# The three products of a split-weight chunk in another order: low weights by high input first, low input last

## The chip, the core and the metric

One core of one Trainium2 chip runs the whole program. The metric is device time in microseconds (us) of one execution. Besides it there is one execution recorded by the hardware profiler, from which all rows below are read. TensorE is called PE in these rows, its weight loads PEld, VectorE DVE, ScalarE ACT, GpSimd POOL, and SyncE, which starts most transfers, SP.

## What is computed

One decoder layer for 256 prompt tokens and 8 single-token sequences, 264 columns in all, in float32:

```python
ada = (c @ w_ada + b_ada)[:, None, :]
sh1, sc1, g1, sh2, sc2, g2 = jnp.split(ada, N_ADA, axis=-1)
u = x * (1 + sc1) + sh1
proj = u @ w_in                                   # 2048 x 8192
z_p, x_c, b_c, c_c, gate_p, gate_c = jnp.split(proj, [o1, o2, o3, o4, o5], axis=-1)
y_p, new_pool = _pool_mixer(z_p, pool_hist, pos, pool_grp_w, pool_scale)
y_p = y_p @ w_pool_up                             # 1024 x 2048
y_c, new_conv = _short_conv(c_c * x_c, conv_hist, conv_w)
y_c = (b_c * y_c) @ w_conv_up                     # 1024 x 2048
mixed = (jax.nn.sigmoid(gate_p) * y_p + jax.nn.sigmoid(gate_c) * y_c) @ w_o   # 2048 x 2048
x = _layernorm(ALPHA * x + g1 * mixed, ln1_g, ln1_b)
u2 = x * (1 + sc2) + sh2
h = jnp.square(jax.nn.relu(u2 @ w_ff1 + b_ff1))   # 2048 x 8192
x = _layernorm(ALPHA * x + g2 * (h @ w_ff2 + b_ff2), ln2_g, ln2_b)            # 8192 x 2048
```

The outputs are the new x of the prompt and of the samples, and the last rows of the pooling and the convolution inputs as new state.

## The kernel before

**Split products.** PE multiplies in a type (float32r) that keeps fewer bits than float32. So each weight tile and each input tile is held as two parts: the high part is the value rounded to that type, the low part is what is left. A product of a weight chunk by an input tile is then three PE products that add up in PSUM: high by high, high by low, low by high. The helper `three` (lines 1590 to 1595) issues them. Each is one weight load of 128 x 128 and one matmul of 128 x 264.

**Units.** The weights are taken in units of 4 chunks (128 rows of the contraction each) by 512 output columns, 1 MB. SP loads a unit into one of four slots of `raw`; ACT writes the high part to `w_hi` (line 715), DVE the low part to `w_lo` (line 1005), each with two slots; PE then runs the helper `unit` (lines 1605 to 1621): for each of 4 output tiles m, which have a PSUM bank each, it runs over the 4 chunks c and calls `three` for each. That makes 4 x 4 x 3 = 48 products in a unit. PE waits once for a unit, for `unit_split`, which DVE raises when both parts are there, and at a bank's first product for `psum_free`. The last of the products of an output tile raises `part_done`, by which DVE or ACT may read the bank, and after the fourth tile ACT and DVE may overwrite the slots.

**Inputs.** An input tile is 264 floats, 1056 bytes, in each partition. `U`, `M` and `H` hold 32, 16 and 32 of them; `M` lies over the upper tiles of `U`. `H` begins 32 tiles behind `U`. The low tile that belongs to a high tile lies:
- 4 tiles further (4224 bytes) for the input projection w_in and for w_ff1, which together make 2 x 64 x 16 = 2048 chunks;
- 8, 16 or 24 tiles away (8448 bytes or a multiple) for the pooling groups, the two up-projections, w_o and w_ff2, which make 16 + 2 x 128 + 256 + 1024 = 1552 chunks.

The first two chunks of the input projection are written out by hand (`first_pair`, lines 1669 to 1687), so that `three` is called for 3598 chunks.

**Stages.** PE runs the conditioning products and the input projection, the pooling groups, the up-projections, w_o, the first normalisation, and then four times 4 blocks of w_ff1 and 4 blocks of w_ff2, each block being 4 units; the second normalisation and the output end it. In a block of w_ff1 the first unit runs in `first_chunks` (lines 1977 to 1987), which goes over the chunks outside and over the output tiles inside. All other units go over output tiles outside. A block of w_ff2 reads input tiles 0 to 3, 4 to 7, 8 to 11 and 12 to 15 of `H` in its four units.

The order of PE's instructions is that in which they are written, in loops of the sequencer.

Of the kernel before, what the change touches and what calls it, by code (L numbers as in the profile page):

```python
# [120 lines left out]
def build_layer(nc, a, o):  # L121
    with ExitStack() as ctx:
# [1464 lines left out]
        def _(pe):  # L1587
            mm = nc.tensor.matmul

            def three(out, w, x_hi, x_lo, start, stop):  # L1590

                wh, wl = w
                mm(out, wh, x_hi, start=start, stop=False)  # L1593
                mm(out, wh, x_lo, start=False, stop=False)  # L1594
                return mm(out, wl, x_hi, start=False, stop=stop)  # L1595

            def w_of(s, c, m, width=UC):

# [6 lines left out]
            def unit(j, n, t0, hi, lo, first=True, last=True, early=None, pieces=None):  # L1605

                if not pieces:
                    pe.wait_ge(unit_split, split_done(n))  # L1610
                for m in range(MT):
                    if pieces:
                        pe.wait_ge(pieces, m + 1)
                    if early and m == MT - 1:
                        early()
                    if first:
                        pe.wait_ge(psum_free, bank_free(t0 + m))
                    for c in range(KC):
                        r = three(bank[m][:, 0:TOK], w_of(j % HL, c, m), tile_of(hi[0], hi[1] + c),
                                  tile_of(lo[0], lo[1] + c), first and c == 0, last and c == KC - 1)  # L1620
                    r.then_inc(part_done, 1)
# [47 lines left out]
            def first_pair():  # L1669

                w = [w_of(0, c, e, HW) for e in range(2) for c in range(2)]
                acc = [bank[e][:, 0:TOK] for e in range(2)]
                pe.wait_ge(u_samples, 1)
                pe.wait_ge(u_hi_ready, 1)
                pe.wait_ge(half_hi, 1)
                for e in range(2):
                    mm(acc[e], w[2 * e][0], U[:, 0, :], start=True, stop=False)
                pe.wait_ge(lo_pieces, 1)
                for e in range(2):
                    mm(acc[e], w[2 * e][1], U[:, 0, :], start=False, stop=False)  # L1680
                pe.wait_ge(u_tile, 1)
                for e in range(2):
                    mm(acc[e], w[2 * e][0], U[:, KC, :], start=False, stop=False)
                pe.wait_ge(u_ready, 1)
                for e in range(2):
                    r = three(acc[e], w[2 * e + 1], U[:, 1, :], U[:, KC + 1, :], False, True)
                r.then_inc(part_done, 1)

            def half_unit(n):

                h = n // HU
                if n == 0:
                    first_pair()
                else:
                    pe.wait_ge(u_ready, h + 1)
                for p in range(1 if n == 0 else 0, PAIRS):
                    pe.wait_ge(lo_pieces, PAIRS * n + p + 1)
                    if PAIRS * n + p >= 2:
                        pe.wait_ge(psum_free, pair_free(PAIRS * n + p))
                    for e, c in ((e, c) for e in range(2) for c in range(2)):  # L1700
                        r = three(bank[p % 2 * 2 + e][:, 0:TOK], w_of(n % HL, c, 2 * p + e, HW), U[:, 2 * h + c, :],
                                  U[:, KC + 2 * h + c, :], c == 0, c == 1)
                    r.then_inc(part_done, 1)
                    if n == 2:
                        hist_sums((2 * p, 2 * p + 1))
# [400 lines left out]
```

## Time and profile before

| what | before |
|---|---|
| median of 3 runs | 1456.91 us (1456.75 to 1457.5) |
| the profiled execution's own time | 1457.35 us |
| its span, first to last instruction | 1455.4 us |
| mean granted PE clock | 0.998 of full speed |
| PE busy | 1438.6 us, 99% of the span, 12268 matmuls |
| weight loads | 1370.0 us, 94%, 12268 loads |
| DVE, ACT, POOL busy | 853.0, 528.3 and 102.5 us |

The mean length of one matmul in the groups of instructions (283 to 285 ns) is from its start to its modelled end; matmuls overlap in the engine, so what a product costs PE is the distance from one start to the next. That is read from the timeline, whose starts are given to 0.01 us: over 48 products that is 0.2 ns for each.

### The profile page before, as it was taken

How to read it: one execution, taken by the hardware profiler on the slowest of the kernel's cores; microseconds unless marked ns; L12 is line 12 of the kernel's file. 1: busy time of each engine (PE TensorE's matmuls, PEld its weight loads, DVE VectorE, ACT ScalarE, POOL GpSimd, SP SyncE). 2: the span in 40 equal slices, each digit the busy share in tenths (PEclk: the TensorE clock that was granted, in tenths of full speed). 3: DMA queues.
4: the chain of work that ended last, by engine and by line, in shares of the span. 5: the costliest groups of instructions: out<-in, count | busy, mean ns of one | idle time of the engine just before them, and what ended most of it. 6: DMA issues, size and time to landing. Idle time of an engine off the chain costs nothing.

```text
span 1455.4 us, 28268 instructions
## 1 busy us (share of the span) xinstructions
PE 1438.6 (99%) x12268; PEld 1370.0 (94%) x12268; DVE 853.0 (59%) x1036; ACT 528.3 (36%) x380; POOL 102.5 (7%) x102
## 2 busy tenths in 40 slices
PE   7999999999999999999999999999999999999998
PEld 6999999998889889897899999999999999999997
DVE  4777666565688656459754545454445544454557
ACT  2333322323335232225534333443334433343435
POOL 1000000000440000000060000000000000000800
PEclk9999999999999999999999999999999999999999
DMA  9988888887886786886765555655556545655541
GB/s 318 382 296 281 300 324 306 308 325 270 328 311 253 279 329 244 338 298 240 248 204 186 189 173 176 180 189 177 175 180 187 179 174 180 187 180 173 182 165 61
DMA packets 150529, 344.71 MB, mean 237 GB/s; under 512 B 6452, under 2 KB 17240, under 8 KB 142105
## 3 DMA queue, kind: packets, MB, share of 16 engines
q1 hardware_dynamic: 148642, 340.36, 68.1%
q0 software_dynamic: 896, 2.36, 0.5%
q8 instruction: 61, 1.00, 0.3%
q10 hardware_dynamic: 912, 0.85, 0.2%
q14 instruction: 18, 0.15, 0.0%
HBM read 341.24 MB, written 2.79 MB: 236 GB/s over the span
## 4 chain that ended last, share of the span: by engine, by line
PE 96%; DVE 2%; DMA 1%; ACT 0%; issue 0%; SPq 0%; DVEq 0%; ACTq 0%
PE main L1593 30%; PE main L1594 30%; PE main L1595 30%; PE ps_ada L1711 1%; PE ps_adat L1711 1%; PE ps_adat L1757 1%; PE ps_a L1711 1%; DMA PB<-in_w_ada 1%; PE ps_ada L1757 1%; DVE w_lo L1005 0%; PE ps_ada L1662 0%; SPq L439 0%; DVE G L1452 0%; PE ps_ada L1649 0%; ACT w_hi L715 0%
## 5 line engine op out<-in xcount | busy, mean ns | idle before, releaser
L715 ACT ACTIVATE w_hi<-raw 128x2048 fp32r<-128x2048 f32 (+1 forms) x227 | 429.7, 1894 | 884.5 <-PE main L1595 871.6
L1005 DVE TENSOR_TENSOR w_lo<-raw,w_hi 128x2048 fp32r<-128x2048 f32 (+1 forms) x212 | 483.3, 2280 | 451.2 <-ACT w_hi L715 450.6
L1593 PE MATMUL main<-U,w_hi 128*128 128x264 f32 x2318 | 660.9, 285 | 3.0 <-issue 1.3
L1595 PE MATMUL main<-U,w_lo 128*128 128x264 f32 x2318 | 658.1, 284 | 0.0
L1594 PE MATMUL main<-U,w_hi 128*128 128x264 f32 x2190 | 619.6, 283 | 0.0
L1593 PEld LDWEIGHTS main<-U,w_hi 128*128 128x128 f32 x2318 | 435.6, 188 | 25.8 <-issue 22.2
L1595 PEld LDWEIGHTS main<-U,w_lo 128*128 128x128 f32 x2318 | 435.0, 188 | 0.0
L1594 PEld LDWEIGHTS main<-U,w_hi 128*128 128x128 f32 x2190 | 411.6, 188 | 0.0
L1593 PE MATMUL main<-H,w_hi 128*128 128x264 f32 x1280 | 364.8, 285 | 0.0
L1595 PE MATMUL main<-H,w_lo 128*128 128x264 f32 x1280 | 362.2, 283 | 0.0
L1594 PE MATMUL main<-H,w_hi 128*128 128x264 f32 x1152 | 327.3, 284 | 0.0
L1593 PEld LDWEIGHTS main<-H,w_hi 128*128 128x128 f32 x1280 | 240.8, 188 | 3.5 <-issue 3.4
L1595 PEld LDWEIGHTS main<-H,w_lo 128*128 128x128 f32 x1280 | 240.4, 188 | 0.0
L1594 PEld LDWEIGHTS main<-H,w_hi 128*128 128x128 f32 x1152 | 216.7, 188 | 0.1
L1594 PE MATMUL main<-M,w_hi 128*128 128x264 f32 x256 | 72.8, 284 | 0.0
L1236 DVE TENSOR_TENSOR PB<-main,PB 128x264 f32<-128x264 f32 x96 | 38.3, 427 | 32.8 <-PE main L1595 32.7
L1236 DVE TENSOR_TENSOR G<-main,G 128x264 f32<-128x264 f32 x96 | 37.6, 427 | 27.2 <-PE main L1595 27.1
L1594 PEld LDWEIGHTS main<-M,w_hi 128*128 128x128 f32 x256 | 48.2, 188 | 0.1
L676 POOL MEMSET Uf<- 128x528 f32 x1 | 0.5, 543 | 594.4 <-PE main L1595 594.4
L1098 DVE TENSOR_TENSOR w_lo<-raw,w_hi 128x512 fp32r<-128x512 f32 x60 | 40.7, 682 | 0.5 <-ACT w_hi L715 0.5
L1352 DVE SCALAR_TENSOR_TENSOR X<-main,ada,X 128x256 f32<-128x256 f32 x72 | 34.1, 480 | 2.4 <-PE main L1595 1.4
L592 POOL TENSOR_TENSOR Uf<-Uf 128x2040 f32<-128x2040 f32 (+3 forms) x4 | 9.4, 2360 | 336.6 <-ACT Uf L817 336.2
(280 smaller groups left out, 636.7 us busy)
## 6 DMA issues: line engine op xcount, KB each, us to landing
raw<-in_w_ff SPq DMA_DIRECT2D x128, 1024.0 KB, 5.2
raw<-in_w_in SPq DMA_DIRECT2D x63, 1024.0 KB, 9.4
ada_raw<-in_w_ada SPq DMA_DIRECT2D x48, 1024.0 KB, 6.6
ada_raw<-in_w_ada SPq DMA_DIRECT2D x36, 512.0 KB, 6.4
raw<-in_w_o SPq DMA_DIRECT2D x16, 1024.0 KB, 9.7
Uf<-in_w_ada SPq DMA_DIRECT2D x10, 1024.0 KB, 10.6
Uf<-in_w_ada SPq DMA_DIRECT2D x16, 512.0 KB, 7.6
raw<-in_w_pool_up SPq DMA_DIRECT2D x8, 1024.0 KB, 9.3
```

Of the source, the lines that this page charges most:

```text
L592: g_tt(dst[:, first:PT, step:PROMPT], src[:, first:PT, step:PROMPT], src[:, first:PT, 0:PROMPT - step], ALU.add)
L676: nc.gpsimd.memset(sum_x, 0.0).then_inc(sum_zeroed, 1)
L715: nc.scalar.activation(w_hi[:, s % HL, 0:size], raw[:, s, 0:size], ACT.Copy).then_inc(hi_ready, 1)
L1005: tt(w_lo[:, s % HL, 0:size], raw[:, s, 0:size], w_hi[:, s % HL, 0:size].bitcast(F32), ALU.subtract).then_inc(unit_split, 1)
L1098: tt(lo, r, hi.bitcast(F32), ALU.subtract).then_inc(lo_pieces, 1)
L1236: tt(dst, bank[m][:, 0:TOK], dst, ALU.add).then_inc(psum_free, 1)
L1352: stt(xt, bank[m][:, 0:PROMPT], gt[:, 0:1], xt, ALU.mult, ALU.add)
L1593: mm(out, wh, x_hi, start=start, stop=False)
L1594: mm(out, wh, x_lo, start=False, stop=False)
L1595: return mm(out, wl, x_hi, start=False, stop=stop)
L1711: r = mm(section_bank[i][BLOCK * j:BLOCK * j + BLOCK, :], c_t[:, k, C_AT:C_AT + BLOCK], blocks[:, j], start=k == 0, stop=k == NT - 1)
L1757: r = mm(group_bank[t][BLOCK * j:BLOCK * j + BLOCK, 0:GROUP_COLS], c_t[:, 2 * n + c, C_AT:C_AT + BLOCK], blocks[:, c, j], start=n == 0 and ...
```

## The change

`three` issues the same three products of the same operands in another order. Before: high weights by high input, high weights by low input, low weights by high input. After: low weights by high input, high weights by high input, high weights by low input. The flags that open and close a sum in PSUM go to the first and the last product as before, and so does the signal at the end of an output tile, which the caller attaches to the product that `three` returns.

```diff
             def three(out, w, x_hi, x_lo, start, stop):
 
                 wh, wl = w
-                mm(out, wh, x_hi, start=start, stop=False)
-                mm(out, wh, x_lo, start=False, stop=False)
-                return mm(out, wl, x_hi, start=False, stop=stop)
+                mm(out, wl, x_hi, start=start, stop=False)
+                mm(out, wh, x_hi, start=False, stop=False)
+                return mm(out, wh, x_lo, start=False, stop=stop)
```

PE's first calls of `three`, at the start of the input projection; each row is a matmul, its output, its input and weights, and what it waits for. Before:

```order
L1593 MATMUL main<-U,w_hi 128x264 [waits u_ready]
L1594 MATMUL main<-U,w_hi 128x264
L1595 MATMUL main<-U,w_lo 128x264
L1593 MATMUL main<-U,w_hi 128x264
L1594 MATMUL main<-U,w_hi 128x264
L1595 MATMUL main<-U,w_lo 128x264
L1593 MATMUL main<-U,w_hi 128x264 [waits lo_pieces]
```

After:

```order
L1593 MATMUL main<-U,w_lo 128x264 [waits u_ready]
L1594 MATMUL main<-U,w_hi 128x264
L1595 MATMUL main<-U,w_hi 128x264
L1593 MATMUL main<-U,w_lo 128x264
L1594 MATMUL main<-U,w_hi 128x264
L1595 MATMUL main<-U,w_hi 128x264
L1593 MATMUL main<-U,w_lo 128x264 [waits lo_pieces]
```

The product with the low weights moved from the third place to the first; the waits stay at the first place. `lo_pieces` is raised by DVE when a piece of the low weights is written, which comes after the high part.

PE at the start of a unit of the convolution's up-projection, where high and low input lie in two tensors (`U` and `H`). Before:

```order
L1593 MATMUL main<-U,w_hi 128x264 [waits psum_free,unit_split,yc_ready]
L1594 MATMUL main<-H,w_hi 128x264
L1595 MATMUL main<-U,w_lo 128x264
L1593 MATMUL main<-U,w_hi 128x264
L1594 MATMUL main<-H,w_hi 128x264
L1595 MATMUL main<-U,w_lo 128x264
```

After:

```order
L1593 MATMUL main<-U,w_lo 128x264 [waits psum_free,unit_split,yc_ready]
L1594 MATMUL main<-U,w_hi 128x264
L1595 MATMUL main<-H,w_hi 128x264
L1593 MATMUL main<-U,w_lo 128x264
L1594 MATMUL main<-U,w_hi 128x264
L1595 MATMUL main<-H,w_hi 128x264
```

The two products with the high input from `U` now stand side by side, and the one with the low input from `H` closes the chunk. The rows of DVE, ACT, POOL and SP are the same before and after, and on PE the number of rows, the lines and the waits at each place too.

## Rows read from the trace of the kernel before

**Rows 1.** The page's head and its first two parts.

```profile
span 1455.4 us, 28268 instructions
PE 1438.6 (99%) x12268; PEld 1370.0 (94%) x12268; DVE 853.0 (59%) x1036; ACT 528.3 (36%) x380; POOL 102.5 (7%) x102
PEclk9999999999999999999999999999999999999999
```

**Rows 2.** The page's chain of work that ended last, by engine.

```profile
PE 96%; DVE 2%; DMA 1%; ACT 0%; issue 0%; SPq 0%; DVEq 0%; ACTq 0%
```

**Rows 3.** Waits: engine, its line, releaser: us in total, times, longest.

```profile
ACT w_hi L715 <- PE main L1595: 871.6, 218, 7.7
DVE w_lo L1005 <- ACT w_hi L715: 450.6, 180, 5.6
PE main L1593 <- DVE w_lo L1005: 1.0, 2, 0.8
```

**Rows 4.** Groups of instructions from the page: busy us, mean ns, idle before.

```profile
L1593 PE MATMUL main<-U,w_hi 128*128 128x264 f32 x2318 | 660.9, 285 | 3.0 <-issue 1.3
L1595 PE MATMUL main<-U,w_lo 128*128 128x264 f32 x2318 | 658.1, 284 | 0.0
L1594 PE MATMUL main<-U,w_hi 128*128 128x264 f32 x2190 | 619.6, 283 | 0.0
L1593 PEld LDWEIGHTS main<-U,w_hi 128*128 128x128 f32 x2318 | 435.6, 188 | 25.8 <-issue 22.2
```

**Rows 5.** Timeline, second w_ff1 stage, third unit of its second block: start us, length.

```profile
921.01 0.28 PE L1593 MATMUL main<-U,w_hi 128*128 128x264 f32 x1
921.01 0.19 PEld L1594 LDWEIGHTS main<-U,w_hi 128*128 128x128 f32 x1
921.13 0.28 PE L1594 MATMUL main<-U,w_hi 128*128 128x264 f32 x1
921.13 0.19 PEld L1595 LDWEIGHTS main<-U,w_lo 128*128 128x128 f32 x1
...
921.38 0.29 PE L1593 MATMUL main<-U,w_hi 128*128 128x264 f32 x1
...
921.74 0.28 PE L1593 MATMUL main<-U,w_hi 128*128 128x264 f32 x1
...
922.09 0.28 PE L1593 MATMUL main<-U,w_hi 128*128 128x264 f32 x1
...
922.46 0.28 PE L1593 MATMUL main<-U,w_hi 128*128 128x264 f32 x1
```

**Rows 6.** Timeline: first products of w_ff1 units, second stage; 48 products between unit starts.

```profile
880.23 0.28 PE L1593 MATMUL main<-U,w_hi 128*128 128x264 f32 x1
...
886.05 0.29 PE L1593 MATMUL main<-U,w_hi 128*128 128x264 f32 x1
...
903.50 0.28 PE L1593 MATMUL main<-U,w_hi 128*128 128x264 f32 x1
...
909.37 0.28 PE L1593 MATMUL main<-U,w_hi 128*128 128x264 f32 x1
...
915.20 0.28 PE L1593 MATMUL main<-U,w_hi 128*128 128x264 f32 x1
...
926.82 0.28 PE L1593 MATMUL main<-U,w_hi 128*128 128x264 f32 x1
```

**Rows 7.** Timeline: the same of w_ff2 units, second stage, and the next w_ff1 start.

```profile
973.46 0.28 PE L1593 MATMUL main<-H,w_hi 128*128 128x264 f32 x1
...
996.76 0.28 PE L1593 MATMUL main<-H,w_hi 128*128 128x264 f32 x1
...
1002.56 0.28 PE L1593 MATMUL main<-H,w_hi 128*128 128x264 f32 x1
...
1008.41 0.28 PE L1593 MATMUL main<-H,w_hi 128*128 128x264 f32 x1
...
1014.21 0.28 PE L1593 MATMUL main<-H,w_hi 128*128 128x264 f32 x1
...
1020.05 0.28 PE L1593 MATMUL main<-H,w_hi 128*128 128x264 f32 x1
...
1066.64 0.28 PE L1593 MATMUL main<-U,w_hi 128*128 128x264 f32 x1
```

## Prediction

> **What bounds the kernel now.** I read the page's head first: PE is busy for 1438.6 of 1455.4 us, at a granted clock in the top tenth in all forty slices, the 2.4 GHz level [rows 1]. The chain that ended last is PE for 96% [rows 2]. The waits say who is ahead: ACT waits for PE to free a slot of the high weights for 871.6 us in 218 waits, DVE waits behind ACT for 450.6, while PE waited for DVE's low weights for 1.0 us, twice [rows 3]. So weights arrive early everywhere, and the time is the sum of what PE's products cost one after the other. For a change inside `three` the question is only what one product costs, and whether it depends on which product stands before it.
>
> The groups give 283 to 285 ns for a matmul at each of the three lines [rows 4], but these overlap. The timeline shows the true distance: matmuls start 0.12 us apart, and the weight load of the next product starts together with the matmul of the one before, also when it loads the same high weights again (921.01 for line 1594) [rows 5]. A load is recorded for every product, the repeated ones too; nothing is skipped (x12268 of both) [rows 1]. From one unit's first product to that of the next there are 48 products. A stage of w_ff1 takes 973.46 - 880.23 = 93.23 us for 768 products, 121.4 ns each; one of w_ff2 1066.64 - 973.46 = 93.18 us, 121.3 ns each [rows 6, 7]. The 10,794 products of `three` (3 x 3598) at 121.4 ns are 1310 us of the 1455.4; the other 145 us are conditioning products, transposes, the few stalls and the two ends, none of which the change touches.
>
> **The change, part by part.** (a) *Number and kind of instructions.* Three loads and three matmuls before and after, of the same shapes, the same weights read twice in a row once per chunk in both orders: before, high weights in places 1 and 2; after, in places 2 and 3. Nothing added, nothing taken away: 0 us.
>
> (b) *Waits.* A unit waits once, at its first product, for both parts of the weights, and the same wait stands there after. In the order before, the high-weight product could in principle have started ahead of the low weights, but it did not: the wait covered both. Where the weights are taken in pieces, at the start of the input projection, `lo_pieces` is again waited for ahead of all three. So DVE's lateness (1.0 us in 2 waits [rows 3]) is paid as before: 0 us. Even if a wait grew by its whole present size again it would be 1 us. The last product of a tile still raises `part_done` at the same place in the stream, so banks and slots come free at the same time, and SP's, ACT's and DVE's queues see the same releases: 0 us. What hides ACT and DVE is their lead on PE of hundreds of microseconds in sum; a change of 0.24 us in when the low weights are read within a chunk does not touch it.
>
> (c) *The spacing of products.* This is the one unknown term. It would be nothing if every product cost the same. It does not. In a unit of w_ff1 the chunks take 0.37, 0.36, 0.35 and 0.37 us in turn (921.01, 921.38, 921.74, 922.09, 922.46) [rows 5]. In w_ff2 the units take 1002.56 - 996.76 = 5.80, then 5.85, 5.80 and 5.84 us, that is 120.8, 121.9, 120.8 and 121.7 ns a product [rows 7]; all are free of waits. The units alternate with the input tiles they read: units one and three read tiles 0 to 3 and 8 to 11, two and four tiles 4 to 7 and 12 to 15. Eight tiles are 8448 bytes, 33 x 256; four tiles are 4224, which leaves 128 over. So I take it, as an estimate from these rows, that the spacing depends on where the input tile lies within some 256 bytes, and on little else.
>
> With that the chunks fall into two classes. For 1552 chunks (4656 products: groups, up-projections, w_o, w_ff2) high and low input lie a multiple of 8 tiles apart, and high and low weights are 16 KB apart. Seen in this way all three products of a chunk read the same places, and the new order is the old one: 0 us. For the 2046 chunks left (6138 products: w_in and w_ff1) the low tile is 128 bytes off. The places read were (a, a+128, a) and become (a, a, a+128): the same three, in another sequence. If a product's cost goes by its own place, the sum stays. The rows support that: two parts of the 120.8 level and one of 121.8 give (2 x 120.8 + 121.8) / 3 = 121.1 ns, and a steady w_ff1 unit pair shows 926.82 - 915.20 = 11.62 us for 96 products, 121.0 [rows 6]. After the change the mixture is the same. I take 0 us for (c).
>
> Bounds from both sides: if the sequence matters, the level could go anywhere that wait-free units show. The lowest is 120.8 [rows 7], which for 6138 products would give (120.8 - 121.1) x 6138 = -1.8 us. The highest is the first unit of the second w_ff1 block, 909.37 - 903.50 = 5.87 us, 122.2 ns [rows 6], which would give +1.1 x 6138 = +6.8 us. I stay at 0 because the mixture reproduces the measured level without any term for the sequence.
>
> Here a rule of the Trainium skill speaks. The rows show 121.4 ns a product with 264 columns, and a spread with the tile read. "TensorE: Matmul & The Clock Gate", Part 2 (step-by-step, and back-to-back issue gap), says that the array has two independent read ports, so that loading the next weights takes nothing from the running matmul, and puts a matmul at its columns by 2.4 GHz plus about 2.5 ns, 112.5 ns here by my working. By that rule the order could not matter at all; the rows differ from it by 9 ns a product, so something of the two reads does interact, and the measurement decides. That gap is why the slower rival below has a chance.
>
> **The rivals.** *Slower: the same input tile twice in a row costs more.* After the change two neighbouring products read the same high tile. Before, this happened only in the unit that goes over chunks outside and output tiles inside, where the last product of one `three` and the first of the next share it. That unit is the slow one in the second block, 5.87 us. Against it: the same unit in the first block of the stage took 886.05 - 880.23 = 5.82 us, 121.2 ns [rows 6], with the same sequence of tiles, so the slow level comes from how the unit is entered, not from the repeat. And w_ff2 units, whose three products all read like places, are not slow. Price +6.8 us: 1463.7. It decides the sign of the result once the spacing grows by 0.5 ns in those 6138 products (3 us).
>
> *Faster: the new sequence falls into the short spacing more often.* One chunk in four of a w_ff1 unit takes 0.35 us, the others 0.36 to 0.37 [rows 5], so a better sequence exists. Were it one chunk more in each four, that is 2046 / 4 = 512 chunks by some 15 ns, -7.7 us: 1449.2. The extreme, all at 0.35 us, is 2046 x 13 ns = -27 us. For it speaks only that nothing rules it out; against it, the mixture argument again.
>
> *The change doesn't do what it says,* or does nothing but reorder: that is the forecast itself. The order of instructions shows the swap in place and no other row moved. A gain from loading the high weights only once would need the second load to vanish; in the kernel before, two neighbouring products had the same weights as well and both loads are there [rows 5], so I give it nothing.
>
> **How the numbers follow.** The sum is made against the profiled execution: 1457.35 us, of which 1455.4 is the span and 1.95 lies around it, 0.44 above the median of 1456.91. The change adds 0 + 0 + 0 us to any of them, so I predict the median, 1456.9. A measurement of this kernel can tell about 0.2% from no change, 2.9 us: 1454.0 to 1459.8. Chances: no difference 0.81; slower by the sequence 0.12; faster by the sequence 0.07. Both ends in term (c) are inside what could happen, and the upper one lies further out, so the range reaches higher than lower: 1453.8 to 1461.0. That holds the forecast's case whole and the weaker half of the slower one.
>
> **What the profile of the changed kernel would show.** For (a): line 1593 with `w_lo`, lines 1594 and 1595 with `w_hi`, the counts of groups unchanged, 12268 loads. For (b): PE's waits for DVE still a microsecond or so, and ACT's wait for PE near 870 us, now under the same line 1595. For (c): w_ff2 units at 5.80 and 5.85 us in turn, unchanged to 0.01 us, since their places are the same; a stage of w_ff2 at 93.18 us. A stage of w_ff1 at 93.2 us within 0.4 (0.5 ns a product). The prediction is wrong if a w_ff1 stage takes 94 us (the slower rival), or 92.4 (the faster one), and the idea of places within 256 bytes falls if w_ff2's units move by more than 0.02 us.

## The result and the profile after

| what | before | after |
|---|---|---|
| median of 22 runs each | 1457.99 us | 1459.74 us |
| ratio after / before | | 1.0014, 95% interval 1.0008 to 1.0019 |
| span of the profiled execution | 1455.4 us | 1457.1 us |

The change makes the kernel slower by 0.14%, 1.75 us at the medians: less than the 0.2% inside which the forecast counted a result as no change, but more than the interval of the ratio leaves to chance. The profiled executions differ by 1.7 us. The rhythm of a unit of products repeats to 0.01 us from unit to unit and from trace to trace, so the traces can say where these are.

The page's head and first parts, and the granted clock, of the changed kernel (answers to [rows 1]); then the waits (answers to [rows 3]), with us in total, times and longest:

```profile
span 1457.1 us, 28268 instructions
PE 1440.1 (99%) x12268; PEld 1371.7 (94%) x12268; DVE 852.7 (59%) x1036; ACT 528.3 (36%) x380; POOL 102.5 (7%) x102
PEclk9999999999999999999999999999999999999999
```

```profile
ACT w_hi L715 <- PE main L1595: 872.8, 218, 7.7
...
PE main L1593 <- DVE w_lo L1005: 1.0, 2, 0.7
```

The same work, the same clock, the same microsecond of waiting for DVE. PE is simply busy for 1.5 us longer. The starts of products in the timeline show in which stage. Four places before: first whole unit of the input projection, first pooling group, first w_ff1 unit, and the last product of the layer.

```profile
123.30 0.29 PE L1593 MATMUL main<-U,w_hi 128*128 128x264 f32 x1
...
461.43 0.28 PE L1593 MATMUL main<-U,w_hi 128*128 128x264 f32 x1
...
688.54 0.36 PE L1593 MATMUL main<-U,w_hi 128*128 128x264 f32 x1 [1.29 <-issue]
...
1440.24 0.28 PE L1595 MATMUL main<-H,w_lo 128*128 128x264 f32 x1
```

The same four places after:

```profile
123.21 0.28 PE L1593 MATMUL main<-U,w_lo 128*128 128x264 f32 x1
...
462.63 0.29 PE L1593 MATMUL main<-U,w_lo 128*128 128x264 f32 x1
...
689.75 0.36 PE L1593 MATMUL main<-U,w_lo 128*128 128x264 f32 x1 [1.44 <-issue]
...
1441.94 0.28 PE L1595 MATMUL main<-H,w_hi 128*128 128x264 f32 x1
```

- Up to the first row: -0.09 us. The first call of `three` comes 1.16 us earlier (22.94 against 24.09 us), and most of that is lost again by this row. In the traces of the ten kernels that carry out the whole layer it lies between 23.9 and 24.3 us in the four with the inputs in the order of before, and between 22.2 and 25.5 in the six with that of after. So single traces differ by more than this at their start.
- Input projection, 50 units, 2400 products: 338.13 us before, 339.42 after, **+1.29**.
- Groups, up-projections, w_o, first normalisation: 227.11 and 227.12, **0.01**.
- w_ff1 and w_ff2: 751.70 and 752.19, **+0.49**.

Within the feed-forward part the second stage shows the units; w_ff1 first (answers to [rows 6]), then w_ff2 (answers to [rows 7]).

```profile
881.57 0.28 PE L1593 MATMUL main<-U,w_lo 128*128 128x264 f32 x1
...
904.90 0.29 PE L1593 MATMUL main<-U,w_lo 128*128 128x264 f32 x1
...
910.72 0.28 PE L1593 MATMUL main<-U,w_lo 128*128 128x264 f32 x1
...
916.56 0.29 PE L1593 MATMUL main<-U,w_lo 128*128 128x264 f32 x1
...
928.24 0.29 PE L1593 MATMUL main<-U,w_lo 128*128 128x264 f32 x1
...
974.92 0.29 PE L1593 MATMUL main<-H,w_lo 128*128 128x264 f32 x1
...
998.22 0.28 PE L1593 MATMUL main<-H,w_lo 128*128 128x264 f32 x1
...
1004.02 0.28 PE L1593 MATMUL main<-H,w_lo 128*128 128x264 f32 x1
...
1009.87 0.28 PE L1593 MATMUL main<-H,w_lo 128*128 128x264 f32 x1
...
1068.10 0.28 PE L1593 MATMUL main<-U,w_lo 128*128 128x264 f32 x1
```

The stage of w_ff2 takes 93.18 us, as before, and its units 5.80 and 5.85, as before. In w_ff1 a steady pair of units takes 928.24 - 916.56 = 11.68 us, 121.7 ns a product, against 121.0 by the rows of before. The first unit of a block goes the other way: 5.82 us, 121.2 ns, against 5.87 (in the first block of a stage, where it took 5.82 before, it now takes 5.81). Together a stage takes 93.35 in place of 93.23. The change cost 0.6 ns a product in w_ff1's steady units, those that follow another unit of their kind. It gave 1 ns back in the first unit of three blocks out of four, and did nothing in w_ff2.

In the input projection the changed kernel has two levels. Here are the starts of two pairs of neighbouring units, the same code on the same layout, with no wait between:

```profile
189.65 0.29 PE L1593 MATMUL main<-U,w_lo 128*128 128x264 f32 x1
...
195.49 0.29 PE L1593 MATMUL main<-U,w_lo 128*128 128x264 f32 x1
...
216.80 0.28 PE L1593 MATMUL main<-U,w_lo 128*128 128x264 f32 x1
...
222.67 0.28 PE L1593 MATMUL main<-U,w_lo 128*128 128x264 f32 x1
```

The first pair lies 5.84 us apart, 121.7 ns a product, the second 5.87 (5.866 before rounding), 122.2 ns. Of the 50 units 22 run at 121.7 ns and 10 at 122.2; the others come behind conditioning products or, one of them, after a short pause, and average more. A level holds until the next conditioning products. In the kernel before, all 30 units that settle do so at 121.1 ns. So in the changed kernel one sequence has two steady rhythms, and the +1.29 us is a mixture of +0.6 and +1.1 ns a product.

### The profile page after: what moved, and what is told of

It reads as the page before. It is cut to its first block, busy times and chain, and to the rows that moved or that the text cites. A ratio compares the mean times of both kernels' runs of the same rounds, so it can differ in the third digit from the quotient of the medians.

```text
span 1457.1 us, 28268 instructions
## 1 busy us (share of the span) xinstructions
PE 1440.1 (99%) x12268; PEld 1371.7 (94%) x12268; DVE 852.7 (59%) x1036; ACT 528.3 (36%) x380; POOL 102.5 (7%) x102
## 4 chain that ended last, share of the span: by engine, by line
PE 95%; DVE 2%; SPq 1%; DMA 1%; ACT 1%; issue 0%; DVEq 0%; ACTq 0%
PE main L1593 30%; PE main L1594 29%; PE main L1595 29%; PE ps_ada L1711 1%; PE ps_adat L1711 1%; PE ps_adat L1757 1%; PE ps_a L1711 1%; DMA raw<-in_w_in 1%; SPq L439 1%; PE ps_ada L1757 1%; DVE w_lo L1005 0%; ACT w_hi L715 0%; PE ps_ada L1662 0%; DVE G L1452 0%; SPq L443 0%
## 5 line engine op out<-in xcount | busy, mean ns | idle before, releaser
L1593 PE MATMUL main<-U,w_lo 128*128 128x264 f32 x2318 | 665.1, 287 | 3.5 <-issue 1.4
```

What stands on the lines that cost most here:

```text
L1593: mm(out, wl, x_hi, start=start, stop=False)
```

## The experiments

**Which of the two sequences matters, weights or inputs?** The change alters both: the weights from (high, high, low) to (low, high, high), the inputs from (high, low, high) to (high, high, low). Two kernels take them apart; each edit is shown against the kernel before.

```diff
-                mm(out, wh, x_hi, start=start, stop=False)
+                mm(out, wl, x_hi, start=start, stop=False)
                 mm(out, wh, x_lo, start=False, stop=False)
-                return mm(out, wl, x_hi, start=False, stop=stop)
+                return mm(out, wh, x_hi, start=False, stop=stop)
```

> Order of the three products: low weights by high input, high weights by low input, high weights by high input. The weights come in the order of the changed kernel, the inputs (high, low, high) in that of the kernel before. Theory A (the spacing goes by the sequence of the places of the input tiles alone): the spacing of the kernel before to 0.01 us, that is first w_ff1 unit of a block 5.86 us, a steady one 5.81, a w_ff1 stage 93.2 us, and a time within 0.5 us of before. Theory B (the spacing goes by which weights come first): the spacing of the changed kernel, first unit 5.81 us, steady ones 5.84, a w_ff1 stage 93.4 us, time +1.5 to 2 us. w_ff2 units 5.80 and 5.85 us by both.

Measured: ratio to before 1.0004 (0.9995 to 1.0013). Unit starts of the second w_ff1 stage:

```profile
880.12 0.28 PE L1593 MATMUL main<-U,w_lo 128*128 128x264 f32 x1
...
903.40 0.28 PE L1593 MATMUL main<-U,w_lo 128*128 128x264 f32 x1
...
909.26 0.28 PE L1593 MATMUL main<-U,w_lo 128*128 128x264 f32 x1
...
915.09 0.28 PE L1593 MATMUL main<-U,w_lo 128*128 128x264 f32 x1
...
926.72 0.28 PE L1593 MATMUL main<-U,w_lo 128*128 128x264 f32 x1
...
973.36 0.28 PE L1593 MATMUL main<-H,w_lo 128*128 128x264 f32 x1
```

First unit 5.86, steady pair 11.63, stage 93.24 us: the kernel before, with the low weights first.

```diff
                 mm(out, wh, x_hi, start=start, stop=False)
-                mm(out, wh, x_lo, start=False, stop=False)
-                return mm(out, wl, x_hi, start=False, stop=stop)
+                mm(out, wl, x_hi, start=False, stop=False)
+                return mm(out, wh, x_lo, start=False, stop=stop)
```

> Order: high weights by high input, low weights by high input, high weights by low input. The inputs come as in the changed kernel (high, high, low), the weights as in neither, and no two neighbouring products of a chunk share weights. Theory A (places of the inputs alone): the spacing of the changed kernel to 0.01 us, first w_ff1 unit 5.81, steady ones 5.84, stage 93.4 us, time +1.5 to 2 us on before. Theory B (which weights come first): the spacing of before, 5.86, 5.81, stage 93.2, time within 0.5 us of before. Theory C (two neighbouring products with the same weights are dearer or cheaper than others): a third spacing, in w_ff2 too.

Measured: ratio 1.0016 (1.0007 to 1.0025).

```profile
881.31 0.28 PE L1593 MATMUL main<-U,w_hi 128*128 128x264 f32 x1
...
904.65 0.29 PE L1593 MATMUL main<-U,w_hi 128*128 128x264 f32 x1
...
910.46 0.28 PE L1593 MATMUL main<-U,w_hi 128*128 128x264 f32 x1
...
916.31 0.29 PE L1593 MATMUL main<-U,w_hi 128*128 128x264 f32 x1
...
927.99 0.29 PE L1593 MATMUL main<-U,w_hi 128*128 128x264 f32 x1
...
974.67 0.29 PE L1593 MATMUL main<-H,w_hi 128*128 128x264 f32 x1
```

First unit 5.81, steady pair 11.68, stage 93.36: the changed kernel, with the high weights first; its input projection has the changed kernel's two levels too. A stage of w_ff2 takes 93.18 us in both kernels. Theories B (weights) and C (repeated weights) fall, and A stands: the sequence of the inputs does it alone. The order of the weights has no effect in this kernel, where high and low weights lie 16 KB apart.

**Do other engines or transfers have a part in it?** A kernel of PE products only, on data that lie still. The core of the helper behind each of its tests; `pairs` and `times` give the 48 products and their repeats:

```python
for m, c in pairs * times:                       # 4 output tiles by 4 chunks, 48 products
    hi, lo = places(c)
    for k, (w, i) in enumerate(order):           # BEFORE = hh, hl, lh   AFTER = lh, hh, hl
        s = (0 if w == "h" else US) + (0 if w_fixed else c * 512 + m * P) + w_shift // 4
        x = (hi if i == "h" else lo) // 4
        mm(bank[m][:, 0:cols], w_all[:, s:s + P], x_all[:, x:x + cols], start=c == 0 and k == 0, stop=c == 3 and k == 2)
```

> Only PE products of 128 x 264 on weights and inputs that lie still, no layer: everything else is left out and the outputs are zeros. Groups of 48 products, one source line for each test: the orders of before, after and the two mixed ones with the low tile 4 tiles (4224 bytes) away, then 8 tiles away, then all inputs at one place (0, 32, ... 224 bytes past a multiple of 256), weights moved by 32, 64 and 128 bytes, the same weights throughout, 256 and 128 columns, and chunks outside. Theory A: without any other engine at work the orders give 121.1 (before) and 121.7 ns (after) as in the kernels, the mixed order with inputs high, low, high the first and with high, high, low the second; 8 tiles away both orders give the same, 120.8 (tiles 0 to 3) and 121.9 (tiles 4 to 7). Single places differ from one another by some ns, between 117 and 125. Theory D (the difference comes from traffic of other engines or transfers beside PE): all orders alike here, and nearer to 117 than to 121.

Its timeline, one row for each test: start, length, line, number of products. L119 is the order of before, L120 that of after, L121 inputs high, low, high with low weights first, L122 inputs high, high, low with high weights first.

```profile
29.29 17.60 PE L119 MATMUL main<-x_all,w_all 128*128 128x264 f32 x144
46.73 17.75 PE L120 MATMUL main<-x_all,w_all 128*128 128x264 f32 x144
64.31 17.64 PE L121 MATMUL main<-x_all,w_all 128*128 128x264 f32 x144
81.80 17.75 PE L122 MATMUL main<-x_all,w_all 128*128 128x264 f32 x144
```

The length of a row runs to the end of its last product, 0.16 us past the next product's start; less that, 17.44, 17.59, 17.48 and 17.59 us for 144 products, 121.1, 122.2, 121.4 and 122.2 ns. With nothing else at work the order of before has its level of the kernel, and the inputs' sequence orders the four (L121 carries a transient from L120 in its first unit). Theory D falls. The size that the expectation gave for the order of after, 121.7 ns, was missed: it is 122.2 here, the level that w_ff1's units of the changed kernel don't have and ten units of its input projection have.

The same run has units whose low tile is 8 tiles away, high and low then a multiple of 256 bytes apart (L123 to L126). Tiles 0 to 3 settle at 5.81 us, 121.1 ns, and tiles 4 to 7 at 5.85, 121.9, in the order of before and in that of after alike. So the 5.80 us of w_ff2's units in the kernel, 120.8 ns, is not the steady level of their place: it is what they cost in turn with the others.

All inputs at one place, two units (96 products) each: L127 at a multiple of 256 bytes, L128 32 bytes further, L131 128, L132 160; L143 has 256 columns, L144 128 columns.

```profile
146.01 11.69 PE L127 MATMUL main<-x_all,w_all 128*128 128x264 f32 x96
157.53 11.84 PE L128 MATMUL main<-x_all,w_all 128*128 128x264 f32 x96
...
192.29 11.81 PE L131 MATMUL main<-x_all,w_all 128*128 128x264 f32 x96
203.94 11.89 PE L132 MATMUL main<-x_all,w_all 128*128 128x264 f32 x96
...
331.90 11.68 PE L143 MATMUL main<-x_all,w_all 128*128 128x256 f32 x96
343.41 10.84 PE L144 MATMUL main<-x_all,w_all 128*128 128x128 f32 x96
354.08 11.91 PE L145 MATMUL main<-x_all,w_all 128*128 128x264 f32 x96
```

Less the same 0.16 us, 120.1, 121.7, 121.4 and 122.2 ns for 264 columns, by the place alone (from start to start L127 is 120.0); 119.9 ns (from start to start) for 256 columns at the place that costs 120.0 with 264; 111.1 ns for 128. Eight columns fewer save nothing, and half the columns save 9 ns. So at 256 to 264 columns it is not the columns that set the rhythm.

**The spacing as a function of places.** The same again with whole blocks, the weights' slots and parts where the kernel has them, and all inputs moved.

> PE products alone again, no layer (everything else is left out, the outputs are zeros), now with the weights' two slots and two parts where the kernel has them, and in the sequence of whole blocks: two w_ff1 blocks (first unit chunks outside, input tiles 8j + c, low tiles 4 further), then two w_ff2 blocks (tiles 4j + c, low tiles 16 further). Each test moves all input tiles by 0, 32, ... 224 bytes, in the order of before and of after, or the weights by 64 or 128 bytes, or takes the chunks in another order. Theory A (the spacing is a fixed function of the sequence of places read): at shift 0 the blocks of the kernels come out to 0.02 us, before 23.32 (w_ff1) and 23.30 (w_ff2), after 23.34 and 23.30, and after minus before is 0.2 to 0.6 ns a product in w_ff1's steady units and 0 in w_ff2; other shifts give other levels, some 0.3 to 1 ns lower, and after can be the faster order at some of them. Theory D (other engines' traffic makes the difference): shift 0 misses the kernels' times by more than 0.5 ns a product and the shifts are alike.

Two w_ff1 blocks, 384 products, in each row. L127: order of before, not moved; L131: inputs moved by 64 bytes; L135: by 128; L143: order of after, not moved; L167: order of before, inputs and weights both moved by 128.

```profile
113.95 46.76 PE L127 MATMUL main<-x_all,w_all 128*128 128x264 f32 x384
...
300.55 47.21 PE L131 MATMUL main<-x_all,w_all 128*128 128x264 f32 x384
...
487.78 46.67 PE L135 MATMUL main<-x_all,w_all 128*128 128x264 f32 x384
...
861.13 46.84 PE L143 MATMUL main<-x_all,w_all 128*128 128x264 f32 x384
...
1981.91 46.79 PE L167 MATMUL main<-x_all,w_all 128*128 128x264 f32 x384
```

Less the 0.16 us again. Not moved: 46.60 us for w_ff1 in the order of before and 46.68 in that of after (the kernels: two blocks of 23.32, 46.64, and of 23.34, 46.68; a first block after w_ff2 is 0.05 shorter in the order of before, in the scan as in the kernel). Moved by 64 bytes: 47.05. By 128: 46.50. With inputs and weights moved alike it is nearly as not moved, 46.63, and the second of the two blocks takes 23.32 us in both. The same holds through the scan: for each of the eight moves, the second w_ff1 block with the weights moved by 128 bytes as well takes, to 0.01 us, what it takes with the inputs alone moved by 128 more, counted round 256; and with the weights alone moved by 64 it takes 23.47 us, as with the inputs alone moved by 192. So in this scan what counts is where the input lies relative to the weights, within 256 bytes.

The single places of the first scan fit that only in part. It also moved the weights by 32, 64 and 128 bytes with all inputs at one place. Of these six tests three settle at the level of the same distance without the weights moved, and three don't: 120.0 ns for 121.0, 120.0 for 121.2, and 123.3 for 120.0 (L136, L137, L139). Whether the way in explains these, or the place of the weights counts by itself as well, no run separates.

The order of after is not the dearer one everywhere: by the second w_ff1 blocks of the scan it is the cheaper at moves of 32, 64 and 192 bytes, and the dearer at the other five.

After's steady units now settle at 121.7 ns, as in w_ff1 of the kernel. In the second scan, further down, the same units with the same layout were entered from other products and settled at 122.2. Of the sixteen pairs of move and order that both scans have, fourteen settle at the same level and two don't: this one, and the order of before at 96 bytes (121.7 and 120.6 ns). So one sequence can have more than one steady rhythm, and what stood before it chooses. The changed kernel shows the same two levels in its input projection.

**The scan's numbers put into the kernel.** Four kernels with one line more, the order of before or after, and 32 or 16 floats of room ahead of the input tensors:

```diff
+        sb("shift", [P, 32])
         at_u = here()
         Uf = sb("Uf", [P, 2 * NT, TOK])
```

> The kernel before, order untouched, with 128 bytes of empty room ahead of the input tensors U, H and G, so that every input tile lies 128 bytes further and the weights stay. Theory A (sequence of places, read off the scan): w_ff1 block 23.26 us in place of 23.32, its steady units 120.6 ns a product, w_ff2 units the other way round, 5.85 and 5.80, the block unchanged; in all 16 x -0.067 for w_ff1 and 2440 x -0.55 ns for w_in, -2.4 us, ratio 0.9983. Theory D (other traffic, or layout doesn't matter): no change.

> The kernel before with 64 bytes of room in that place. Theory A: w_ff1 block 16 x +0.22 = +3.5 us, w_in +1.67 ns x 2440 = +4.1, w_ff2 +0.49 ns x 3072 = +1.5, up-projections and w_o +0.75: +9.9 us, ratio 1.007, with w_ff1's steady units at 122.8 ns a product. Theory D: no change.

> The changed kernel with the same 64 bytes. Theory A: w_ff1 +1.2, w_in +1.4, w_ff2, up and w_o +2.3: +4.8 us on the kernel before, so 5 us faster than the order of before at the same place: the change of order is then a gain. Theory B or C (the new order costs by itself, wherever the tiles lie): 2 us slower than the order of before at the same place.

> The changed kernel with 128 bytes. Theory A: w_ff1 +2.45 us, w_in +2.7, the rest 0: +5.2 us on the kernel before, 7.6 us slower than the order of before at the same place. Theory B or C: 2 us slower than that.

| kernel | ratio to before (95%) | expected by A | second w_ff1 block, us: scan, kernel |
|---|---|---|---|
| before, moved by 128 | 0.9977 (0.9968 to 0.9986) | 0.9983 | 23.25, 23.25 |
| before, moved by 64 | 1.0068 (1.0052 to 1.0083) | 1.007 | 23.54, 23.54 |
| after, moved by 64 | 1.0033 (1.0021 to 1.0045) | 1.0033 | 23.39, 23.39 |
| after, moved by 128 | 1.0024 (1.0015 to 1.0034) | 1.0036 | 23.47, 23.47 |

The block's times are the distance between two w_ff1 blocks' first products; for before moved by 64 they can be read here:

```profile
909.65 0.28 PE L1594 MATMUL main<-U,w_hi 128*128 128x264 f32 x1
...
933.19 0.28 PE L1594 MATMUL main<-U,w_hi 128*128 128x264 f32 x1
```

This is the decisive comparison. At 64 bytes the order of after is the faster one, by 5.1 us at the medians (1462.56 against 1467.66); at 128 it is the slower one by 6.7 us (1461.43 against 1454.72); not moved, by 1.75. The new order has no cost of its own: whether it costs or saves depends on where the tiles lie. The last kernel came out 1.4 us short of the expected +5.2; its feed-forward part is exact (+2.5 us). Of the shortfall 0.9 us lies ahead of the first whole unit of the input projection, which it reached at 122.41 us in place of 123.30, and 0.6 in that projection (+2.1 in place of +2.7), which the scan had not imitated. At 64 bytes the projection fell short as well, +3.3 us in place of +4.1 in the order of before and +1.1 in place of +1.4 in that of after, and the start was 0.5 us longer in both: part of the agreement of these two totals is luck. What the scan did imitate came out: the feed-forward part is +5.0 and +2.7 us, as expected. The start varies from trace to trace, as said above; why was not looked into.

**The cheapest sequence.** A second scan over places, orders of the inputs and orders of the chunks.

> PE products alone (no layer; everything else is left out, the outputs are zeros), to look for the cheapest sequence: for the input tiles moved by 0, 32, ... 224 bytes, the six orders of the chunks that begin with chunk 0, and the three orders of a chunk's inputs (high, low, high; high, high, low; low, high, high), three units as w_ff1's later ones each; then four units as w_ff2's for moves 0 to 96 and the six chunk orders. Theory A (a fixed function of the sequence of places): levels spread from about 120 to 123 ns a product, with 120.5 or less for some. The floor is what one place for all gave, 120.0 ns, since 256 columns cost as much as 264 there: the loading of weights sets it. Theory D: no spread.

It found steady levels from 120.0 to 124.4 ns. The only one at 120.0 for the low tile 4 tiles away was this row: the order of after, inputs moved by 192 bytes, chunks 0, 2, 1, 3:

```profile
2063.18 17.45 PE L239 MATMUL main<-x_all,w_all 128*128 128x264 f32 x144
```

17.28 us from its first product to that of the next test, for 144 products. That the loading of weights sets this floor, as the expectation has it, is an inference from 256 and 264 columns costing the same; no run tests it. Built into the kernel, on top of the changed one (shortened: the flag that closes a sum goes to the last chunk of the new order, and `n_is_far` is true for units whose low tile is 4 tiles further):

```diff
+        sb("shift", [P, 48])
...
-                    for c in range(KC):
+                    chunks = (0, 2, 1, 3) if lo[0] is U and hi[0] is U and n_is_far(lo[1], hi[1]) else (0, 1, 3, 2)
+                    for c in chunks:
```

> The cheapest sequence of the second scan put into the kernel: order of the changed kernel (low weights by high input, high by high, high by low), input tensors moved by 192 bytes, chunks in the order 0, 2, 1, 3 in the units whose low tile is 4 tiles further (w_in from its sixteenth unit on, w_ff1's later three units) and 0, 1, 3, 2 in the others; w_ff1's first unit keeps its order. Theory A: if the units settle as in the scan, 120.0 ns in w_in and w_ff1 in place of 121.1: 2440 + 2304 products x -1.1 ns = -5.2 us, others -0.13 ns x 4656 = -0.6, w_ff1's first unit unknown (+-0.8): 1452 +-1, ratio 0.996. If a unit's level hangs on how it is entered, as the scans showed for the changed order at no move (121.7 or 122.2), w_ff1 may settle at another level, up to 122, and the gain is down to that of w_in, or nothing.

> The same with the chunks 0, 2, 1, 3 in w_ff1's first unit too. Theory A: as the kernel without it to 1 us, apart from the level of that unit (768 products) and of what follows it.

The first: ratio 0.9981 (0.9972 to 0.9990), half of what was hoped. The third and fourth units of w_ff1's blocks did reach 120.0 (926.62 - 915.10 = 11.52 us for two units):

```profile
915.10 0.28 PE L1594 MATMUL main<-U,w_lo 128*128 128x264 f32 x1
...
926.62 0.28 PE L1594 MATMUL main<-U,w_lo 128*128 128x264 f32 x1
```

In the input projection nine units reached 120.0 as well, and twenty-one ran at 121.7, so nothing was gained there on the kernel before (338.23 us against 338.13). The second, which differs only in the chunk order of w_ff1's first unit: ratio 1.0008 (0.9999 to 1.0017), its third and fourth units at 121.7 ns; the expectation that it would match the first to 1 us, but for these units, left that open. The two kernels differ by 3.7 us at the medians. Here the same code of a unit runs at 120.0 or 121.7 ns by what ran before it. The two fastest kernels of the study are the kernel before with the inputs moved by 128 bytes (1454.72 us against 1457.59 for before in its comparison, 0.23% faster) and the first of these two (1454.73 against 1457.32); their intervals overlap, so the study doesn't rank them. Both beat both kernels of the case.

## Why the prediction was wrong

**What held.** The bound (PE, product after product) and the view it was read from. Term (a): nothing added or taken away. Term (b): waits, releases and the other engines as before, the wait for the low weights 1.0 us in both. The classes of term (c): for the 4656 products whose parts lie a multiple of 256 bytes apart the forecast was no change to 0.01 us, and it came so in w_ff2, and within 0.01 us over groups, up-projections and w_o together. A w_ff1 stage at 93.35 us also lies within the 0.4 us that the forecast allowed it: the signs of being wrong that it named, 94 and 92.4 us, were set wider than the effect, and so was its 0.2% for what a measurement can tell. With 22 runs of each kernel the interval is 0.05% to either side.

**The step that failed** is the value taken in term (c) for the other 6138 products: "If a product's cost goes by its own place, the sum stays", supported by a mixture of two levels that came to 121.1 ns. It does not go by its own place alone. Two arrangements of the same three places cost 121.1 and 121.7 ns, or 122.2 by the way in. That the mixture hit the level of before was chance. The 120.8 ns that it used is not the level of a place: products alone on tiles 0 to 3, high and low at like places, settle at 121.1, which makes the mixture (2 x 121.1 + 121.9) / 3 = 121.4. And with the levels of w_ff2's units in the moved kernels the same mixture would give (2 x 122.2 + 121.4) / 3 = 121.9 ns at 64 bytes, where 122.8 was measured, and (2 x 121.9 + 120.8) / 3 = 121.5 at 128, where it was 120.6. The size: +0.54 ns on average over 2400 products of the input projection, 1.29 us, and +0.49 us net in the feed-forward part: together +1.8 us where 0 stood. The bounds given for the term (-1.8 to +6.8 us) held it, and so did the range, though 122.2 ns is not the dearest that the same products can be (122.8 at 64 bytes). The value chosen between them was wrong, and with it the sign. The rows to choose by were there: w_ff1's first unit at 121.2 in one block and 122.2 ns in the next, with the same products, says that history counts. The text used that row only against a rival.

**The slower rival** named the right term and the wrong mechanism. The same high tile twice in a row is not dear: w_ff1's first unit, where it happened three times in a chunk before and happens four times after, became faster with the change, and at 64 bytes the sequence with the repeat is the cheaper one in every steady unit of w_ff1 (121.7 against 122.8 ns).

**The faster rival**, a sequence that falls into the short spacing more often, was right that such sequences exist (120.0 and 120.6 ns), though this change was not one.

**The rule of the skill.** By the Trainium skill, "TensorE: Matmul & The Clock Gate", Part 2, step-by-step, loading the next weights takes no read bandwidth from a running matmul, and by its back-to-back issue gap a matmul of 264 columns would take 112.5 ns by my estimate. The same section says that this formula is for a matmul by itself, and for a stream of loads and matmuls it gives about 81 ns at 128 columns and about 131 at 512; the prediction left that out. In the runs products alone on the chip take 120.0 to 124.4 ns by place, order and way in, 256 columns take as long as 264, and 128 columns 111.1. The measurement decides: moving the weights alone changes the block's time as moving the inputs alone does (23.47 us in place of 23.32), so the reads of weights and of inputs are not independent in these runs. The prediction argued this from the 9 ns between 112.5 and 121.4, which by themselves could have had other causes.

## What to carry to other kernels

Where PE runs without a gap, what is left to measure is the distance between starts of products, and 48 products at 0.01 us show 0.2 ns. There, a reordering or a move of a buffer that adds and removes nothing was worth 0.1 to 0.7% either way: before giving an order credit or blame, try it at a second placement, and scan placements with products alone. One execution of the scan reproduced the kernel's w_ff1 blocks to 0.01 us; for the input projection, whose surroundings it did not imitate, it was off by up to 0.8 us. Don't average levels of different sequences; if two blocks of the same code have different levels, the rhythm has a memory.

## What was not expected of the hardware

- Products of 128 x 128 weights by 264 columns start 0.11 to 0.13 us apart in a pattern that repeats from unit to unit and from trace to trace. It hangs on where input tiles lie relative to the weights, within 256 bytes: second w_ff1 blocks of 23.25 to 23.54 us by the move in the order of before, with all eight moves repeated when the weights move along. Three single-place tests of another scan don't fit that rule.
- 256 columns cost 119.9 ns and 264 columns 120.0 at the same place, 128 columns 111.1: between 256 and 264 the columns don't set the pace.
- The same sequence of reads can settle in two rhythms by what ran before it: 120.0 or 121.7 ns a product in the kernel of the cheapest sequence, 121.7 or 122.2 in the changed kernel. Which mechanism in the chip does this the runs don't say.
